# Up matrices of a mixture-of-experts stage: one 2 MB transfer each, awaited and released whole, instead of 1 MB halves

## The reference, cut to what matters

```python
e_ids = g_sel[:, None] * EXPERTS_PER_GROUP + top_i          # 640 tokens, 2 experts each
combine = jnp.sum(one_hot(e_ids, N_EXPERTS) * w_sel[..., None], axis=1)
for e in range(N_EXPERTS):
    h = silu(xt @ w1[e]) * (xt @ w3[e])                     # w1, w3: 1024 x 512, the up matrices
    y = y + combine[:, e:e + 1] * (h @ w2[e])               # w2: 512 x 1024, the down matrix
```

## Time and profile before

| what | value |
|---|---|
| median of 3 runs | 1352.26 us (1347.19 to 1352.87) |
| the profiled execution | 1352.2 us, its span 1350.4 us |
| PE busy | 1188.1 us, 88% of the span |
| DVE, ACT, POOL busy | 490.8, 275.2, 361.7 us |
| mean granted clock of TensorE | 0.93 |
| DMA | 204.32 MB, mean 151 GB/s |
| stage 5 on PE | from 977 to 1315 us |

### The profile page before, as it was taken

The page is one execution under the profiler, slowest core; times in us unless marked ns, Lnnn a source line. Parts: engine busy times, 40 slices in busy tenths (PEclk is TensorE's granted clock), DMA queues, the critical chain, the costliest instruction groups (busy, mean ns, idle before and its releaser), DMA issues. The chain is left out here.

```text
span 1350.4 us, 19239 instructions
## 1 busy us (share of the span) xinstructions
PE 1188.1 (88%) x6804; PEld 868.7 (64%) x6805; DVE 490.8 (36%) x967; ACT 275.2 (20%) x612; POOL 361.7 (27%) x221
## 2 busy tenths in 40 slices
PE   1899999999999999888998999998289999999770
PEld 1797989888888888758998899545233333333220
DVE  5425465546555665566004112111511111111115
ACT  2122323232322232341112000022011111110002
POOL 4431515241424241024665466000011111111003
PEclk9988999989998999788999899999599999999885
DMA  5250332323232322013225422591289958169966
GB/s 169 83 164 26 88 98 69 103 64 102 63 103 64 102 64 71 1 47 124 71 69 152 121 68 60 205 359 46 93 334 399 396 210 295 47 238 398 396 249 241
DMA packets 186078, 204.32 MB, mean 151 GB/s; under 512 B 13399, under 2 KB 132183, under 8 KB 186022
## 3 DMA queue, kind: packets, MB, share of 16 engines
q1 hardware_dynamic: 176422, 178.62, 38.8%
q10 hardware_dynamic: 5840, 12.06, 3.3%
q0 software_dynamic: 3760, 12.85, 2.6%
HBM read 180.63 MB, written 22.69 MB: 151 GB/s over the span
## 5 line engine op out<-in xcount | busy, mean ns | idle before, releaser
L1692 PE MATMUL bank<-w,xe 128*64 128x512 f32 x864 | 203.2, 614 | 16.6 <-DMA w<-in_w 14.3
L177 POOL TENSOR_TENSOR wh<-raw,zcol 128x1024 fp32r<-128x1024 f32 x40 | 77.1, 1929 | 336.0 <-DMA raw<-in_w_in 257.9
L1692 PEld LDWEIGHTS bank<-w,xe 128*64 128x64 f32 x864 | 61.0, 141 | 135.4 <-issue 120.3
L599 PE MATMUL bank<-xh,wh 128*128 128x320 f32 x384 | 125.9, 328 | 0.0
L600 PE MATMUL bank<-xl,wh 128*128 128x320 f32 x384 | 122.5, 319 | 0.0
L601 PE MATMUL bank<-xh,wl 128*128 128x320 f32 x384 | 122.3, 319 | 0.0
L1720 PE MATMUL bank<-w,hT 128*64 128x512 f32 x432 | 99.0, 601 | 4.0 <-ACT hT L1752 4.0
L599 PE MATMUL bank<-wh,xh 128*128 128x256 f32 x320 | 96.4, 301 | 5.7 <-POOL xpad L582 5.7
L180 POOL TENSOR_TENSOR wl<-raw,wh 128x1024 fp32r<-128x1024 f32 x40 | 97.2, 2429 | 3.1
L600 PE MATMUL bank<-wl,xh 128*128 128x256 f32 x320 | 93.1, 291 | 0.0
L601 PE MATMUL bank<-wh,xl 128*128 128x256 f32 x320 | 93.0, 291 | 0.0
(11 more groups left out here) (269 smaller groups left out, 2092.2 us busy)
## 6 DMA issues: line engine op xcount, KB each, us to landing
w<-in_w SPq DMA_DIRECT2D x64, 1024.0 KB, 15.2
w<-in_w SPq DMA_DIRECT2D x16, 2048.0 KB, 17.4
raw<-in_w_in SPq DMA_DIRECT2D x40, 512.0 KB, 4.9
kc<-in_cache_k SPq DMA_DIRECT2D x8, 1024.0 KB, 5.5
vc<-in_cache_v SPq DMA_DIRECT2D x8, 1024.0 KB, 5.8
wraw<-in_w_in SPq DMA_DIRECT2D x16, 512.0 KB, 3.6
block_outputs<-yb ACTq DMA_DIRECT2D x54, 128.0 KB, 5.4
block_outputs<-zero ACTq DMA_DIRECT2D x19, 256.0 KB, 5.0
```

Source lines behind the costliest of these rows:

```text
L177: nc.gpsimd.tensor_tensor(wh[:, :, j, :], r[:, :, :], zcol[:, 0:1].rearrange("p (a b) -> p a b", a=1) .to_broadcast([P, KT, P]), ALU.add). ...
L599: nc.tensor.matmul(out, ah, bh, start=(k == 0), stop=False)
L1692: mm = nc.tensor.matmul(up_bank[j * BT:(j + 1) * BT, :].rearrange("p (m f) -> p m f", m=2), xe[:, col:col + BT], w13[par][:, :, c, j * HC: ...
```

## The change

The halves go. `load13` issues w1 and then w3 of an expert in one 2 MB transfer each; there is one arrival semaphore for each slot and one release semaphore. PE waits once, ahead of chunk 0, for both matrices (the awaited value stays 32 for each use of the slot: two transfers of 16), and releases once, after chunk 7. SP waits once for each expert, for that release, then issues both, and goes on to w2 as before. ACT's wait is on the one semaphore, at the same event as before. Bytes, slots, the order of the blocks and the products stay as they were.

```diff
-    w13_in = [[sem(f"w13_in{half}{i}") for i in range(WBUF)] for half in range(2)]
+    w13_in = [sem(f"w13_in{i}") for i in range(WBUF)]
...
-    def load13(eng, e, par, half):
-
-        k = slice(half * KT // 2, (half + 1) * KT // 2)
+    def load13(eng, e, par):
+
         for j, src in enumerate((w1s, w3s)):
-            eng.dma_start(w13[par][:, j, k, :], src[bass.ds(e, 1), :, k, :].rearrange("o p k f -> p (o k) f")) \
-                .then_inc(w13_in[half][par], 16)
+            eng.dma_start(w13[par][:, j, :, :], src[bass.ds(e, 1)].rearrange("o p k f -> p (o k) f")) \
+                .then_inc(w13_in[par], 16)
...
-                for half in range(2):
-                    sp_.wait_ge(free13[half], n)
-                    load13(sp_, e, par, half)
+                sp_.wait_ge(free13, n)
+                load13(sp_, e, par)
                 sp_.wait_ge(free2, n)
                 load2(sp_, e, par, w2_in[par])
...
-                half = c // (UPC // 2)
-                if c % (UPC // 2) == 0:
-                    pe.wait_ge(w13_in[half][par], n * 32)
+                if c == 0:
+                    pe.wait_ge(w13_in[par], n * 32)
...
-                if c % (UPC // 2) == UPC // 2 - 1:
-                    mm.then_inc(free13[half], 1)
+                if c == UPC - 1:
+                    mm.then_inc(free13, 1)
...
-                act.wait_ge(free13[1], S.b + 1)
+                act.wait_ge(free13, S.b + 1)
```

More of the change, by code:

```diff
@@ L1343, in _ @@
             for e in range(2):
-                load13(sp_, e, e, 0)
-                load13(sp_, e, e, 1)
+                load13(sp_, e, e)
                 load2(sp_, e, e, w2_in[e])
@@ L1593, in build_rest @@
     xt_done, xe_ready = sem("xt_done"), sem("xe_ready")
-    free13, free2 = [sem(f"free13_{half}") for half in range(2)], sem("free2")
+    free13, free2 = sem("free13"), sem("free2")
     th_ready, s_ready, gg_ready = sem("th_ready"), sem("s_ready"), sem("gg_ready")
@@ L1628, in _ @@
         def _(sp_):
-            load13(sp_, 2, 2, 0)
-            load13(sp_, 2, 2, 1)
+            load13(sp_, 2, 2)
             load2(sp_, 2, 2, w2_in[2])
```

## The result

The changed kernel takes 1358.35 us (median of 20 runs, 1351.85 to 1365.83); the kernel before, in 20 runs, 1351.8 (1347.19 to 1355.94). The ratio is 1.0048, 95% interval 1.0030 to 1.0066: some 6.5 us slower, against +6.0 forecast.

A forecast was written before the change was run, and what follows sets the result against it. PE was taken to bound stage 5 from 1100 to 1186 us and DMA from 1220 to 1300; 6.05 - 0.35 + 0.3 = +6.0 on 1352.2 gave 1358.2 us, with an 8-in-10 range of 1352.0 to 1362.0.

The forecast's parts named there:

- Removed: Stage 5: 32 transfers, 16 release waits of SP and PE's wait at chunk 4 go; none stands on the path.
- The wait that moves: Tail of stage 5: block 26 starts when all 4 MB have landed, not the first half; +6.05 us, the main term.
- That the delays of blocks 23 to 25 do not add up: Tail: delays of 5.3, 6.0 and 5.9 us add nothing, because each next block waits for its own weights again.
- The clock of block 26: Block 26 runs slow as today after its gap, but at a mean clock-drop cost of 2.25 us against 2.6; -0.35 us.
- the one I chose: Clock in the tail: drops at the gaps before blocks 23, 24 and 26, is kept at the 3.0 us gap before 25.
- The full-clock rival: Block 26: the gap before block 24 keeps the clock, so block 26 saves 2.6 us; 1356.0 us, chance 0.15.
- The later release: SP issues expert 10's loads at about 1191.5 instead of 1187.3 us, covered by its w2's later wait; cost nothing.
- The carry: Expert 10's later loads: if the cover up to its w2's wait is short, about 1 us is carried on.
- The middle: PE-bound stretch: block 4 waits for expert 4's last load if it is that expert's first block; +0.3 us.
- the 1.4 us to spare at block 22: Expert 11's last load lands at 1227.1 us, 1.4 us ahead of block 22's start at 1228.53.
- Twice the size: Tail's ten pairs: 2 MB instead of 1 MB loads leave the stream's rate as it is; 0, ends -8 and +4 us.

The follow-up runs named there:

- experiment 1: The kernel before, with PE waiting for both halves of an expert ahead of chunk 0; 1 MB loads and release by halves stay; ratio 1.0038 to the kernel before.
- experiment 2: The kernel before, with SP waiting for the second half's release before it issues either half of an expert; ratio 0.9998 to the kernel before.
- 4: The changed kernel, with PE's loop written out for experts 13 to 15 and expert 15 alone loaded and awaited by halves; ratio 1.0033 to the kernel before.
- experiment 6: The changed kernel with the loop written out and expert 15 alone by halves, timed once more; ratio 1.0009 to the kernel before.
- 9: The kernel before, loop written out for experts 13 to 15, PE waiting whole for all experts but 14 and 15; ratio 1.0011 to the kernel before.
- experiment 3: The changed kernel, with each expert's up matrices in four loads of 1 MB; wait and release stay whole; ratio 1.0060 to the kernel before.
- 5: The changed kernel, with PE's loop written out for experts 13 to 15 and every expert whole; ratio 1.0029 to the kernel before.
- experiment 8: The changed kernel's whole up matrices, with SP issuing the up loads of expert e+1 ahead of w2 of expert e; ratio 1.0012 to the kernel before.

## Why the prediction was right, step by step

**Removed.** The list has 16 release waits of SP; it is 13, one for each of experts 3 to 15, since experts 0 to 2 are loaded without one. Nothing hangs on it.

**The wait that moves** (+6.05). Right in place and size. From t0 block 26 starts 7.08 us later (321.39 - 314.31). Of this 0.83 is the delay that PE brings from block 4, which starts 49.74 us behind t0 against 48.90, and the rest, 6.25, is the second half's landing instead of the first's, with 0.2 of a later stream. Experiments 1 and 2 show that the wait alone does it (+7.1) and the release alone does not (+0.3). From the issue of expert 10's w2 to block 26's start it was 1305.88 - 1214.59 = 91.3 us; 91 was forecast.

**That the delays of blocks 23 to 25 do not add up** held in the changed kernel. Experiments 4, 6 and 9 show the limit of the step: take block 26's wait away and block 25's comes forward: block 26 then starts 3 to 4 us later than before, part of it by the written-out loop.

**The clock of block 26** (-0.35). The direction was right, the size small: 5.35 instead of 6.21 for its first half, -0.86. The pattern was not the one I chose: all four gaps, 5.46, 3.82, 4.15 and 3.95, dropped the clock, each at a cost of 1.75 to 2.0 us. These rows of the changed kernel show it behind the gaps of blocks 24 and 26 (columns as in the earlier trace rows):

```profile
1271.50:1275.00 3.50, 3.50 (x10) 1.11 (x12) 0.00 (x0) 0.00 (x0) 0.00 (x0) 0.54 1.03 413
...
1306.00:1309.00 3.00, 3.00 (x8) 0.91 (x10) 0.00 (x0) 0.00 (x0) 0.00 (x0) 0.50 1.03 411
```

The full-clock rival is the pattern that experiments 1 and 3 ran, with the same whole wait, so it is no alternative to the forecast's cause. There is one profile of the changed kernel; which pattern its timed runs took is not shown.

**The later release** (0). Right by experiment 2. The carry that I bounded at 1 us was 0.2 for the stream.

**The middle** (+0.3). The place was right, block 4, which starts as expert 4's last up load lands, so it is that expert's first block. The size was 0.83 in this profile, because that load landed 0.6 us later than before against t0 (49.7 against 49.1). The wait there was 0.66 here, 0.29 in experiment 1, 0.15 in 3, 0.34 in 4 and 5, 0.93 in 6, and too short to be listed in 9, so 0.3 lies inside its scatter. Wrong was the 1.4 us to spare at block 22: it waited 0.22 us here, as expert 11's last up load landed 2.6 us later against t0 than before, though not in the other kernels with whole waits. It cost nothing, since block 23 waits for its own weights behind it.

**Twice the size** (0). Right: expert 14's and expert 15's last up loads land 17.3 us apart, as before, and 1 MB loads gave no shorter time (experiment 3). The Trainium skill's page "DMA: Bandwidth & Descriptors", section "Bandwidth", has larger transfers faster; this trace does not show it for loads that are queued behind each other. Both figures that the prediction took from that page of the Trainium skill, for the rate and for the fixed 2 us, are given there for transfers that GpSimd issues, while SP issues the loads here.

Sum from t0 to the last down product: 7.08 - 0.86 = +6.22, forecast +6.0. The main term was right by its mechanism. That the sum comes so close is in part luck: block 4 cost 0.53 us more than its term and the clock gave back 0.51 more than its term, and the two cancel. The timed runs alone could not tell: their interval is 4.1 to 8.9 us.

## What to carry to other kernels

Where a queue of loads is the bound, look at the size of what is awaited before the size of a load. Here 1 MB against 2 MB for each load made no difference that shows, and the wait did: the consumer of the last load starts later by what lies between its first usable part and its whole. Price that from the landing times of the last block, and check which block comes forward when its wait is gone. What helped here was the order: loads in the order in which they are needed, and none stuck behind a wait that belongs to another.

## What the runs showed of the hardware

- The length of a gap alone does not decide the clock. Gaps of 3.02 to 3.36 us (the latter in experiment 6) left it at full speed in some places, and one of 3.19 kept it in experiment 1 (first half 3.65, in the rows above) and dropped it in experiment 8 (granted clock 1.00 and 0.71 in 3 us behind them):

```profile
1244.43 5.35 PE L1694 MATMUL bank<-w,xe 128*64 128x512 f32 x16 [3.19 <-DMA w<-in_w]
```

- Ahead of stage 5, where only unchanged work runs apart from the loads of experts 0 to 2, t0 lay anywhere from 970.7 to 984.5 us in the twelve profiles. In the changed kernel's, the granted clock from 400 to 600 us was 0.88 (first row), in the one before 0.91 (second row); the rest of that scatter was not looked into:

```profile
400.00:600.00 200.00, 189.11 (x1146) 161.29 (x1144) 106.37 (x216) 62.71 (x148) 42.81 (x20) 0.88 0.19 54
```

```profile
400.00:600.00 200.00, 185.52 (x1150) 157.31 (x1149) 110.40 (x221) 64.89 (x152) 44.09 (x22) 0.91 0.20 58
```
